# Two-sided mixers: the norm of the differential queries and keys per token tile, tile 0 one projection earlier, the engines' orders laid anew

## The reference

```python
def rms_norm(x, gain):
    y = x * lax.rsqrt(jnp.mean(x * x, axis=-1, keepdims=True) + RMS_EPS)
    return y * gain

def diff_attention(q, k, v, q_gain, k_gain, ..., cos, sin):   # 4 heads, d = 32
    def prep(t, g):                                            # 2 * 4 parts of 32 for q, as many for k
        return partial_rope(rms_norm(t.reshape(B, S, 2 * H, d), g), cos, sin, d // 4)
    s = jnp.einsum('ibhqd,ibhkd->ibhqk', q12, k12) * d ** -0.5
    p = jax.nn.softmax(s, axis=-1)
    a = p[0] - lam * p[1]
    return jnp.einsum('bhqk,bhkd->bhqd', a, v)

for l in range(2):
    x = x + 0.5 * swiglu(rms_norm(x, ffn1_norm[l]), ...)
    na_q, ..., dl_v = split(rms_norm(x, mix_norm[l]) @ w_in[l])
    o = concat(neighborhood(...), diff_attention(...), gqa_axial(...), dilated(...))
    x = x + o @ w_out[l]
    x = x + 0.5 * swiglu(rms_norm(x, ffn2_norm[l]), ...)
```

## Time and profile before

| | us |
|---|---|
| median of 3 runs | 1625.03 |
| lowest, highest | 1624.77, 1627.66 |
| span of the profiled execution | 1624.4 |
| PE, DVE, ACT, POOL busy in it | 1587.5, 1081.0, 867.5, 97.7 |
| mean granted clock of PE | 0.996 |

### The profile page before, as it was taken

The page is one execution under the profiler, slowest core; times in us unless marked ns, Lnnn a source line. Parts: engine busy times, 40 slices in busy tenths (PEclk is TensorE's granted clock), DMA queues, the critical chain, the costliest instruction groups (busy, mean ns, idle before and its releaser), DMA issues.

```text
span 1624.4 us, 21699 instructions
## 1 busy us (share of the span) xinstructions
PE 1587.5 (98%) x7988; PEld 1313.4 (81%) x7988; DVE 1081.0 (67%) x1764; ACT 867.5 (53%) x1643; POOL 97.7 (6%) x159
## 2 busy tenths in 40 slices
PE   8999999999999999999899999999999989999998
PEld 7888887688888888887678888888888879878886
DVE  7767677676767766678676766658654566675454
ACT  7444567654435444467664444767444466674342
POOL 0000022100000000020210000011000000110000
PEclk9999999999999999999999999999999999999999
DMA  9878743277877777764158876633665545256551
GB/s 368 295 285 281 201 143 130 91 261 264 277 272 198 266 266 273 258 161 137 56 200 275 287 270 204 196 118 130 207 197 180 185 159 174 84 181 224 191 180 54
DMA packets 96567, 332.12 MB, mean 204 GB/s; under 512 B 14544, under 2 KB 15056, under 8 KB 95952
## 3 DMA queue, kind: packets, MB, share of 16 engines
q1 hardware_dynamic: 77184, 276.87, 51.3%
q10 hardware_dynamic: 19280, 53.88, 10.1%
HBM read 329.64 MB, written 1.06 MB: 204 GB/s over the span
## 4 chain that ended last, share of the span: by engine, by line
PE 92%; DVE 3%; POOL 2%; DMA 2%; ACT 1%; issue 1%; DVEq 0%; POOLq 0%; SPq 0%; ACTq 0%
PE PS L849 27%; PE PS L851 26%; PE PS L850 26%; PE PS L927 2%; PE PS L1029 2%; DMA raw<-in_ffn 2%; PE PS L1050 1%; PE PS L1092 1%; POOL st L2191 1%; PE PS L1188 1%; PE PS L1189 1%; PE PS L1190 1%; PE PS L867 1%; DVE Wl L1715 1%; PE PS L1072 1%
## 5 line engine op out<-in xcount | busy, mean ns | idle before, releaser
L1715 DVE TENSOR_TENSOR Wl<-raw,Wh 128x1024 fp32r<-128x1024 f32 (+1 forms) x298 | 348.6, 1211 | 29.0 <-ACT Wh L1325 28.2
L849 PE MATMUL PS<-Wh,Hh 128*128 128x512 f32 (+1 forms) x824 | 322.7, 392 | 4.9 <-DVE Hl L1775 3.9
L851 PE MATMUL PS<-Wh,Hl 128*128 128x512 f32 (+1 forms) x824 | 319.0, 387 | 0.0
L850 PE MATMUL PS<-Wl,Hh 128*128 128x512 f32 (+1 forms) x824 | 318.7, 387 | 0.0
L1325 ACT ACTIVATE Wh<-raw 128x1024 fp32r<-128x1024 f32 (+1 forms) x298 | 297.5, 1047 | 13.2 <-PE PS L851 8.4
L1715 DVE TENSOR_TENSOR QTl<-raw,QTh 128x1024 fp32r<-128x1024 f32 (+1 forms) x196 | 230.1, 1206 | 26.3 <-ACT QTh L1325 26.0
L1411 ACT ACTIVATE WK<-PS,st 128x256 f32<-128x256 f32 x88 | 41.6, 474 | 331.2 <-PE PS L851 331.2
L849 PE MATMUL PS<-QTh,Hh 128*128 128x512 f32 (+2 forms) x536 | 209.5, 391 | 2.5 <-DVE Hl L1775 1.7
L851 PE MATMUL PS<-QTh,Hl 128*128 128x512 f32 (+2 forms) x536 | 207.1, 386 | 0.0
L850 PE MATMUL PS<-QTl,Hh 128*128 128x512 f32 (+2 forms) x536 | 207.0, 386 | 0.0
L1325 ACT ACTIVATE QTh<-raw 128x1024 fp32r<-128x1024 f32 (+1 forms) x196 | 196.9, 1045 | 8.4 <-PE PS L851 4.7
(11 more groups left out here) (241 smaller groups left out, 2263.4 us busy)
## 6 DMA issues: line engine op xcount, KB each, us to landing
raw<-in_ffn SPq DMA_DIRECT2D x396, 512.0 KB, 5.4
BT<-in_ada ACTq DMA_DIRECT2D x96, 512.0 KB, 4.3
raw<-in_win SPq DMA_DIRECT2D x64, 512.0 KB, 4.9
raw<-in_wo SPq DMA_DIRECT2D x32, 512.0 KB, 5.3
raw<-in_win SPq DMA_DIRECT2D x8, 420.0 KB, 4.0
raw<-in_lat SPq DMA_DIRECT2D x6, 512.0 KB, 6.2
BT<-in_nab SPq DMA_DIRECT2D x2, 1024.0 KB, 7.0
raw<-in_win SPq DMA_DIRECT2D x8, 256.0 KB, 2.9
```

What stands on the lines that cost most here:

```text
L849: e.matmul(out_, xh, wh, start=start, stop=False)
L850: e.matmul(out_, xh, wl, start=False, stop=False)
L851: return e.matmul(out_, xl, wh, start=False, stop=stop)
L1715: ins = e.tensor_tensor(low(p)[:, 0:w], raw[p % RAW][:, 0:w], high(p)[:, 0:w].bitcast(f32), ALU.subtract)
```

## The change

Group 3's norm is made in two events, `norm 3, 0` and `norm 3, 1`, one for each tile: one square on ACT, a sum of 16 heads on DVE (`st` columns of that tile alone), a root of 16 columns on POOL. Tile 0's event stands ahead of `proj 4, 1` on ACT and ahead of the pieces of `parts 25` on DVE; tile 1's stands right behind `turn_qk 2` on both. The rope waits for both roots. Groups 0 to 2 are as before. The orders around it are written anew:
- PE: `proj 5, 1` stands between `S 5` and `V 3`, not behind `T 4`.
- ACT: `N 3` ahead of `V 2`, `E 4` ahead of `T 3` and `proj 5, 0`, `proj 5, 1` behind `E 5`; the pieces are made at `parts` 26, 27, 29, 31, 32 and no longer at 26, 28, 30, 32.
- DVE: of the three pieces that stood at `parts 28` ahead of the norm, one stands behind `S 4` and two behind `turn_qk 3`; `N 4` ahead of `T 3`; `turn_qk 3` and the two pieces ahead of `N 5`.

```diff
@@ PE
-  ("V", 3, 0, 0), ("T", 4, 0, 0), ("proj", 5, 1, 0), ("turn_qk", 3, 0, 0), ("V", 4, 0, 0), ("T", 5, 0, 0),
+  ("proj", 5, 1, 0), ("V", 3, 0, 0), ("T", 4, 0, 0), ("turn_qk", 3, 0, 0), ("V", 4, 0, 0), ("T", 5, 0, 0),
@@ ACT
-  ("V", 1, 0, 0), ("parts", 26, 0, 0), ("proj", 4, 1, 0), ("turn_qk", 2, 0, 0), ("parts", 28, 0, 0),
-  ("norm", 3, 0, 0), ("V", 2, 0, 0), ("N", 3, 0, 0), ("proj", 5, 0, 0), ("T", 3, 0, 0), ("E", 4, 0, 0),
+  ("V", 1, 0, 0), ("norm", 3, 0, 0), ("parts", 26, 0, 0), ("proj", 4, 1, 0), ("turn_qk", 2, 0, 0),
+  ("norm", 3, 1, 0), ("N", 3, 0, 0), ("V", 2, 0, 0), ("parts", 27, 0, 0), ("E", 4, 0, 0), ("T", 3, 0, 0),
...
@@ def norm_qk (DVE)
-  e.wait_ge(g_sq, 8 * l + 2 * x + 2)
-  e.tensor_reduce(st[:, SS:SS + 2 * nh], NW[:, 0:2 * nh * n].rearrange("p (h n) -> p h n", n=n),
+  a, b = norm_heads(x, y)
+  e.wait_ge(g_sq, 8 * l + 2 * x + norm_tiles(x, y)[-1] + 1)
+  e.tensor_reduce(st[:, SS + a:SS + b], NW[:, a * n:b * n].rearrange("p (h n) -> p h n", n=n),
@@ def rope_qk
-  e.wait_ge(g_rs, 4 * l + x + 1)
+  e.wait_ge(g_rs, 5 * l + x + 1 + (x == 3))
@@ pool_program
-  root(0, 2 * GROUPS[x][1], GROUPS[x][2]).then_inc(g_rs, 1)
+  root(*norm_heads(x, y), GROUPS[x][2]).then_inc(g_rs, 1)
```

More of the change, by code:

```diff
@@ L135, in walk @@
                 ("E", 2, 0, 0), ("T", 1, 0, 0), ("N", 2, 0, 0), ("proj", 4, 0, 0), ("E", 3, 0, 0), ("T", 2, 0, 0),
-                ("V", 1, 0, 0), ("parts", 26, 0, 0), ("proj", 4, 1, 0), ("turn_qk", 2, 0, 0), ("parts", 28, 0, 0),
[3 rows of a table removed]
+                ("V", 1, 0, 0), ("norm", 3, 0, 0), ("parts", 26, 0, 0), ("proj", 4, 1, 0), ("turn_qk", 2, 0, 0),
+                ("norm", 3, 1, 0), ("N", 3, 0, 0), ("V", 2, 0, 0), ("parts", 27, 0, 0), ("E", 4, 0, 0), ("T", 3, 0, 0),
+                ("proj", 5, 0, 0), ("N", 4, 0, 0), ("V", 3, 0, 0), ("parts", 29, 0, 0), ("T", 4, 0, 0), ("E", 5, 0, 0),
+                ("proj", 5, 1, 0), ("turn_qk", 3, 0, 0),
[1 row of a table added]
                 ("V", 5, 0, 0), ("chunks", 0, 0, 0), ("N", 6, 0, 0), ("chunks", 1, 0, 0), ("T", 6, 0, 0), ("E", 7, 0, 0),
@@ L159, in walk @@
                 nxt[1], ("parts", 36, 0, 0), ("res", s, 1, 0), ("parts", 39, 0, 0)],
-            "POOL": [("norm", 0, 0, 0), ("norm", 1, 0, 0), ("norm", 2, 0, 0), ("norm", 3, 0, 0), ("sums", 0, 0, 0),
+            "POOL": [("norm", 0, 0, 0), ("norm", 1, 0, 0), ("norm", 2, 0, 0), ("norm", 3, 0, 0), ("norm", 3, 1, 0), ("sums", 0, 0, 0),
                 ("sums", 1, 0, 0), ("res", s, 0, 0), ("res", s, 1, 0)],
@@ L607, in program, with norm_tiles, norm_heads @@
         GROUPS = ((0, 8, 64, range(0, 4)), (512, 8, 64, range(4, 8)), (1024, 6, 64, range(8, 11)), (1408, 16, 32, range(11, 15)))
+        def norm_tiles(x, y):
+            return (y,) if x == 3 else (0, 1)
+        def norm_heads(x, y):
+            nh = GROUPS[x][1]
+            return (y * nh, y * nh + nh) if x == 3 else (0, 2 * nh)
         TAB = {1: (4, 16, 1024), 2: (4, 64, 1152), 3: (8, 8, 1664)}
@@ L1495, in project_a, with norm_qk @@
                     e.activation(VF[:, y, 640:896], src[:, 0:256], ACT.Copy, scale=r).then_inc(j_act, 1)
-            def norm_qk(stage, x):
+            def norm_qk(stage, x, y):
                 l = stage[1]
                 c0, nh, n, _ = GROUPS[x]
-                for t in range(2):
+                for t in norm_tiles(x, y):
                     e.wait_ge(j_act, act_steps(stage, (0, 1, 3, 4)[x], t))
                     if t == 0 and x:
-                        e.wait_ge(g_sum, 4 * l + x)
+                        e.wait_ge(g_sum, 5 * l + x)
                         e.wait_ge(g_rope, 3 * l + x - 1)
@@ L1657, in act_program @@
                     elif what == "norm":
-                        norm_qk(stage, x)
+                        norm_qk(stage, x, y)
                     elif what == "turn_qk":
@@ L1936, in lam, with norm_qk @@
                 e.tensor_reduce(st[:, LA:LA + 2], lt, AX.X, ALU.add).then_inc(lam_sum, 1)
-            def norm_qk(stage, x):
+            def norm_qk(stage, x, y):
                 l = stage[1]
                 c0, nh, n, _ = GROUPS[x]
-                e.wait_ge(g_sq, 8 * l + 2 * x + 2)
-                e.tensor_reduce(st[:, SS:SS + 2 * nh], NW[:, 0:2 * nh * n].rearrange("p (h n) -> p h n", n=n),
+                a, b = norm_heads(x, y)
+                e.wait_ge(g_sq, 8 * l + 2 * x + norm_tiles(x, y)[-1] + 1)
+                e.tensor_reduce(st[:, SS + a:SS + b], NW[:, a * n:b * n].rearrange("p (h n) -> p h n", n=n),
                                 AX.X, ALU.add).then_inc(g_sum, 1)
                 if x == 0:
-                    e.wait_ge(g_sum, 4 * l + 1)
+                    e.wait_ge(g_sum, 5 * l + 1)
                     root(0, 2 * nh, n).then_inc(g_rs, 1)
@@ L2245, in pool_program @@
                         if x:
-                            e.wait_ge(g_sum, 4 * k + x + 1)
-                            root(0, 2 * GROUPS[x][1], GROUPS[x][2]).then_inc(g_rs, 1)
+                            e.wait_ge(g_sum, 5 * k + x + y + 1)
+                            root(*norm_heads(x, y), GROUPS[x][2]).then_inc(g_rs, 1)
                         else:
```

## The result

| | before | after |
|---|---|---|
| median of 13 runs each, us | 1626.11 | 1629.13 |
| lowest, highest | 1624.68, 1627.87 | 1627.91, 1630.12 |
| span of the profiled execution | 1624.4 | 1627.0 |
| mean granted clock of PE in it | 0.996 | 0.992 |

The ratio is 1.0019 with a 95% interval of 1.0012 to 1.0025: the kernel became 3.0 us slower. The forecast was 1624.0 with a range up to 1627.0, so the time lies above the range. What happened is in kind rival C (a longer stretch at the low clock behind the gap), which had a chance of 0.10 and a price of 1627.4.

A forecast was written before the change was run, and what follows sets the result against it. TensorE, busy 1587.5 of 1624.4 us, bounds the kernel, so only its waits or low clock can go. Two mixers at 0.5 us give 1.0 off, 1623.4 in the profile and 1624.0 as median; range 1620.8 to 1627.0.

The forecast's parts named there:

- rival C: Behind the gap before T 5: two clock falls in a row, a further 3.4 us at 1.2 GHz; 1627.4 us, chance 0.10.
- step 1: Group 3's norm: halving it brings GpSimd's roots at 268.7 to 270.6, removing VectorE's 1.98 us wait at the rope.
- step 2: VectorE's queue: rope at 270.65 to 273.5, maxima of S 5 done by 274.7, this work 4.3 us earlier.
- step 3: TensorE: proj 5,1 before V 3 costs nothing extra; T 4's wait goes, turn_qk 3's two become 0.3 and 0.15 us.
- step 4: Before T 5: N 5, late behind two weight pieces, makes one 3.25 us wait; T 5 starts at 281.45, not 282.10.
- step 5: TensorE's clock: falls once per mixer near 281; 0.65 us won, S 6 loses about 0.35; 0.5 taken per mixer.
- step 6: DMA: the next stage's first two loads go out some 13 us later, still before they are wanted; costs nothing.
- the gain of 1.0 us: Whole kernel: 0.5 us won in each of two mixers, 1.0 us off the profiled 1624.4.
- A: Clock stays high through T 5 and S 6 despite the gap: 2.8 us won for both mixers; 1620.5 to 1622.2, chance 0.15.
- B: N 5 is not late, so T 5 does not wait: 8.0 us won, 1617; chance 0.05.
- the third fall: Clock drop at 792 to 796 in before's second mixer; 1.7 us more won if it goes too.
- D: VectorE's tile 0 sum holds up V 2 or S 4: 0.1 to 0.3 us per mixer; chance counted within the forecast's 0.70.

The follow-up runs named there:

- e1: The changed kernel with N 5 ahead of the two weight pieces on VectorE instead of behind them; 1620.2 us.
- g2: The changed kernel with E 5 ahead of T 4's copy on ScalarE, and N 5 directly behind that copy on both ScalarE and VectorE; 1621.0 us.
- e4: The kernel before with the new orders but group 3's norm left whole; 1630.5 us.
- e7: The kernel before with unused zero matmuls filling TensorE's waits ahead of T 4 and both halves of turn_qk 3; 1623.5 us.
- e8: The changed kernel with unused zero matmuls filling TensorE's waits ahead of T 5, V 5 and S 8; 1623.4 us.
- g1: The changed kernel with E 5 ahead of T 4's copy on ScalarE, N 5 earlier on both engines and VectorE's two pieces separated; 1617.8 us.
- e5: The kernel before with VectorE's two weight pieces moved from ahead of the norm to ahead of N 5; 1628.0 us.
- e6: The changed kernel with one weight piece ahead of N 5 on VectorE and the other behind it; 1624.2 us.

## Why the prediction was wrong, point by point

**The norm in halves (step 1): right.** GpSimd's two roots, each 16 columns, and VectorE's rope in after:

```profile
261.46 3.21 POOL L2200 TENSOR_TENSOR st<-st,mhalf 128x16 f32<-128x16 f32 x1
...
266.74 2.90 POOL L2200 TENSOR_TENSOR st<-st,mhalf 128x16 f32<-128x16 f32 x1
```

```profile
270.55 0.69 DVE L1914 COPY PF<-PS 128x512 f32<-128x512 f32 x1
271.16 1.22 DVE L1968 TENSOR_TENSOR A<-A,st 128x1024 f32<-128x1024 f32 x1
```

They took 3.21 and 2.90 us, between the bounds of 2.7 and 3.75; the second ends at 269.64, or 269.0 without the 0.6 us of later start, in the range of 268.7 to 270.6 and before the rope wants it. The 1.98 us wait is gone. The contention that the Trainium skill (GPSIMD Engine Reference, Key points) describes, GpSimd against VectorE instructions with two SBUF inputs, would have put the root at the late end; here it came near the early one. Nor do the three powers of 16 columns follow it: VectorE subtracted low parts, two inputs each, beside about 2.3 us of the one that took 3.21 us, 1.2 us of the one that took 2.90, and 1.0 us of before's, which took 3.75.

**VectorE's order (step 2): right.** Rope at 270.65 was forecast and 271.16 measured, 270.53 without the later start; behind it the maxima of S 5 start at 274.01, or 273.4, forecast 273.5.

**proj 5,1 (step 3): right.** It waits for nothing, T 4 does not wait, and turn_qk 3 waits 0.34 and 0 us where 0.3 and 0.15 were forecast.

**T 5 late next (step 4): right in kind and size.** Forecast 3.25 us, measured 3.12, released by ScalarE's N 5, whose reciprocal follows directly on the two pieces (281.10). e1 shows that the pieces make 1.8 us of it. The other 1.3 us stay with N 5 ahead of the pieces and go when E 5 stands ahead of T 4's copy on ScalarE (g2); e4 shows that the split has no part in it.

**The clock (step 5): the step that failed.** I took it that the gap brings one fall as before, near 281, so that T 5 runs slow and S 6 wholly at the low clock for 0.35 us more. Instead, in the first mixer, the clock fell 3 us later, at 284.0: T 5 ran fast, S 6 started 1.3 us sooner than before, counted from V 2, and then the clock stayed low for 10.2 us, which by S 9 had turned the 1.3 us won into 0.6 lost. In the second mixer it fell at 785.8, as T 5 started, and stayed low for 13.7 us.

Two things were mis-sized. First the length: 3.4 us in each mixer were forecast, 10.2 and 13.7 came, also against before's 3.4 and 6.8. Second the gain under it. The forecast's own terms, 0.65 us won at T 5 less 0.35 for S 6, make 0.3 per mixer and not the 0.5 that went into the sum; and S 6 wholly at the low clock takes 2.07 us (second mixer) against before's 1.28, so that term is 0.8 and not 0.35. With the clock out of the way the new orders are worth 0.2 us by the medians and nothing by the traces (e7, e8): T 5 comes 0.2 us sooner after V 2 in e8 than in e7, V 5 0.5 us later, and T 6 at the same time, 26.98 and 26.99 us after V 2. The step had named the piece that ScalarE now has ahead of T 5's copy, and put it at nothing: it is what V 5 waits 0.59 us for in e1. By the medians the sum of the two is 0.2 us won, 3.2 lost.

**DMA (step 6): nothing, as forecast.** The loads that go out later are wanted behind the mixer, and there after loses nothing: from the end of the first mixer to V 2 of the second it stays 1.2 to 1.3 us behind before.

**The rivals.** C had the mechanism and the sign: it decides "if the low clock is still there at 285", and the window 284 to 288 reads 0.50. The prediction also named the sign: low for more than 3.5 us at one place. C's price was 3.4 us more at 1.2 GHz per mixer, 1.7 us each. The extra stretch was twice that, 6.8 us per mixer (23.9 less 10.2, halved), and each us of it cost 0.24 or less and not 0.5. In part that is because the slower PE hides waits that the other engines would make it do (e1's 0.59 and 0.62 us before V 5 and S 8 are 0.33 and nothing in after); that this is all of it is not shown. The two errors nearly cancelled in the price by luck, 3.4 against 3.2 by the medians. What made the range miss was the gain of 1.0 us, of which at most 0.2 was there, the median of before, which is 1.1 us higher over 13 runs than over the 3 that I added the 0.6 from, and a chance of 0.10 for the case that came. The text had its own evidence for C, the second mixer of before with two falls within 14 us, and gave it too little. A (the gap without the fall) and B (T 5 not late) were no outcomes of this change, but e8 and g1 made them: e8, with the gap filled and no fall, lies 2.7 us below before (V 2 to S 9: 3.5), where A had 2.8 without the third fall and 4.5 with it; g1 lies 8.4 below, where B had 8.0. D did not happen: V 2 and S 4 were not held up.

**What stays open.** Why the clock stays at 1.2 GHz for 10 or 14 us while PE is busy. The matmuls in these stretches (scores with 32 rows, values with 64 columns, full projections) are not enough to bring it down: in e1 the same ones run at 2.4 GHz from end to end. Nor is it settled why one wait of 1.61 us (e5) stood ahead of 10.2 us in one mixer and of none in the other, or why runs of one program differ in it (e6). The lengths in the table are those of one execution each.

## What to carry to other kernels

When a change gathers several short waits of TensorE into one long one, price the clock behind it as its own term: take its length from no single stretch of the trace of before (there it was 3.4 us at a time, and 10.2 and 13.7 came), and its cost per us from what the other engines would make TensorE wait anyway. Ask of every step that is moved off a wait whose cover it loses: two weight pieces that were free under GpSimd's wait cost 8.9 us when they stood ahead of the softmax that the next transposes need, some 3.6 of them by the wait and the rest by the clock; in before's order the same two cost 1.8 (e5). To tell a wait from the clock behind it, fill the wait with idle matmuls: the order of all real work stays, and what the time loses is the clock.
